# RG-LRU stage of a fused retention / RG-LRU trunk step: next x projection before the gates, gate projection after them, output projection tile by tile

## The reference, cut to what matters

```python
gate_in, x_in = jnp.split(h @ lru_w_in[o], 2, axis=-1)         # two projections, 1024 -> 1024 each
xc = centred_dwconv(x_in, lru_conv_w[o], lru_conv_b[o])         # 4 taps along the tokens, per channel
# rg_lru_dir, once forward and once on the flipped sequence:
r  = sigmoid(block_diag_linear(xc, wa, ba))                     # 8 blocks of 128 x 128
ig = sigmoid(block_diag_linear(xc, wx, bx))
log_a = -LRU_C * r * softplus(-lam)
a, mult = exp(log_a), sqrt(-expm1(2.0 * log_a))
h_t = a_t * h_{t-1} + (mult * (ig * xc))_t                      # a scan along the tokens
mix = (gelu(gate_in) * (h_f + flip(h_b))) @ lru_w_out[o]
x = x + g1 * mix
```

## Time and profile before

| | us |
|---|---|
| three runs | 2728.86, 2735.11, 2736.41 (median 2735.11) |
| the profiled execution, its own time | 2731.88 |
| span of its trace | 2730.1 |
| PE busy in it | 2609.2 (96%) |
| DVE busy | 1641.1 (60%) |
| ACT busy | 666.3 (24%) |
| POOL busy | 699.7 (26%) |

### The profile page before, as it was taken

How to read it: one execution, slowest core, us unless ns; L and a number is a source line. 1 busy time by engine, 2 the same in 40 slices (tenths; PEclk the granted TensorE clock), 3 DMA queues, 4 the chain that set the end, 5 groups by cost and what they waited for, 6 DMA issues and landing times.

```text
span 2730.1 us, 39975 instructions
## 1 busy us (share of the span) xinstructions
PE 2609.2 (96%) x14730; PEld 2524.3 (92%) x14730; DVE 1641.1 (60%) x3056; ACT 666.3 (24%) x1016; POOL 699.7 (26%) x395
## 2 busy tenths in 40 slices
PE   7999999899999999999999889789999999999998
PEld 4999999899999999999998778678999999999997
DVE  5878778548567567567586777855433443442444
ACT  5323323232001001001044544423110110110113
POOL 0221212222222222222223323432222232222321
PEclk9999999999999999999999989899999999999998
DMA  6422222312222222222222101121111111111111
GB/s 235 146 70 69 82 67 71 124 47 66 63 81 69 64 82 69 61 85 69 62 73 104 38 21 36 59 77 31 47 39 42 43 38 46 38 44 41 38 46 70
DMA packets 259139, 181.18 MB, mean 66 GB/s; under 512 B 9205, under 2 KB 253685, under 8 KB 258166
## 3 DMA queue, kind: packets, MB, share of 16 engines
q1 hardware_dynamic: 257924, 169.99, 20.4%
q10 hardware_dynamic: 1138, 10.21, 1.0%
HBM read 165.48 MB, written 14.69 MB: 66 GB/s over the span
## 4 chain that ended last, share of the span: by engine, by line
PE 85%; DVE 9%; issue 3%; ACT 2%; DMA 0%; ACTq 0%; DVEq 0%; POOL 0%; POOLq 0%; SPq 0%
PE psum L588 80%; PE psum L862 2%; DVE mod_sum L1228 2%; DVE work_f L1624 1%; DVE h_lo L1254 1%; DVE sumsq L1197 1%; PE mod_psum L613 1%; DVE x L1275 1%; PE psum L668 1%; DVE sumsq L1260 1%; DVE h_hi L1598 1%; DVE mod_sum L1223 0%; DVE s_bwd L1474 0%; PE psum L743 0%; ACT rate_f L1107 0%
## 5 line engine op out<-in xcount | busy, mean ns | idle before, releaser
L588 PE MATMUL psum<-h_hi,w_hi 128*128 128x384 f32 (+1 forms) x2880 | 682.0, 345 | 36.4 <-DVE h_lo L1254 25.6
L531 POOL CAST w_hi<-w_raw 128x1024 fp32r<-128x1024 f32 x184 | 193.5, 1052 | 1886.9 <-PE psum L588 1041.1
L588 PE MATMUL psum<-h_lo,w_hi 128*128 128x384 f32 (+1 forms) x2880 | 666.1, 340 | 0.0
L588 PE MATMUL psum<-h_hi,w_lo 128*128 128x384 f32 (+1 forms) x2880 | 663.7, 339 | 0.0
L588 PEld LDWEIGHTS psum<-h_hi,w_hi 128*128 128x128 f32 x2880 | 520.2, 191 | 48.7 <-issue 23.3
L1275 DVE SCALAR_TENSOR_TENSOR x<-psum,mod,x 128x768 f32<-128x768 f32 (+2 forms) x432 | 238.5, 610 | 476.8 <-PE psum L588 476.8
L588 PEld LDWEIGHTS psum<-h_lo,w_hi 128*128 128x128 f32 x2880 | 524.4, 190 | 0.0
L588 PEld LDWEIGHTS psum<-h_hi,w_lo 128*128 128x128 f32 x2880 | 521.3, 190 | 0.0
L533 POOL TENSOR_TENSOR w_lo<-w_raw,w_hi 128x1024 fp32r<-128x1024 f32 x184 | 445.6, 2422 | 14.7
L978 ACT ACTIVATE relu<-relu,bias 128x384 f32<-128x384 f32 x128 | 72.0, 610 | 1211.1 <-DVE relu L1326 1211.1
L588 PE MATMUL psum<-hid_hi,w_hi 128*128 128x384 f32 x1536 | 351.8, 336 | 2.8 <-DVE x L1275 2.8
(11 more groups left out here) (223 smaller groups left out, 1886.7 us busy)
## 6 DMA issues: line engine op xcount, KB each, us to landing
w_raw<-in_mlp_w SPq DMA_DIRECT2D x128, 512.0 KB, 4.0
mod_raw<-in_mod_w SPq DMA_DIRECT2D x160, 256.0 KB, 2.9
w_raw<-in_ab_w_in SPq DMA_DIRECT2D x24, 512.0 KB, 4.5
x_spill<-x ACTq DMA_DIRECT2D x2, 4608.0 KB, 13.9
w_raw<-in_lru_w_in SPq DMA_DIRECT2D x16, 512.0 KB, 4.1
x<-x_spill SPq DMA_DIRECT2D x2, 2880.0 KB, 9.6
x_rows<-in_x_sample SPq DMA_DIRECT2D x8, 512.0 KB, 7.4
scale_raw<-in_mod_w SPq DMA_DIRECT2D x8, 512.0 KB, 14.4
```

The source lines that it names most:

```text
L531: pool.tensor_copy(w_hi[:, s, :], w_raw[:, s, :]).then_inc(hi_done, 1)
L588: mm = pe.matmul(psum[:, s, c, 0:end - c * CH], w, v[:, k, c * CH:end], start=(first and n == 0 and w is hi[k] and v is in_hi), stop=(last ...
```

## The change

The order of PE becomes: x projection of block 0; then for each block b: x projection of b+1, gates of b, gate projection of b (the last block has no next x). The convolution accumulates in a tile of its own, `xc_next`; ACT does its first tap with the bias (`conv_start`) and, later in the block, copies `xc_next` to `xc` (`take_xc`), which gates and `block_products` read. DVE begins a block with the convolution of b+1 and evicts the gate projection of b between the two directions. ACT makes `h_hi` of all eight `mix` tiles after its last block; POOL makes the low parts of tiles 0 to 4, DVE those of 5 to 7. `out_proj`, in both layers, does each early input tile for c = 0 and then for c = 1. SP's and POOL's orders follow. Cut to its core:

```diff
-DVE_LOW = 2
+POOL_LOW = 5
+        xc_next = tile_at(9, "xc_next")
...
+            load_unit(None, 0, U1, cols(a["lru_w_in"][0], D_MODEL))
+            with sp.Fori(0, KT - 1) as b:
+                load_unit(b, BLK_UNITS, U1 + 1, cols(a["lru_w_in"][0], b * P + (P + D_MODEL)))
+                load_gates(b)
+                load_unit(b, BLK_UNITS, U1 + 2, cols(a["lru_w_in"][0], b * P))
...
             def block_products(b, last):
-                pool.wait_ge(xc_ready, b + 2)
+                pool.wait_ge(xc_copied, b + 1)
...
             split(first + KT - 1, 0)
+            block_products(KT - 1, True)
             split(first + KT - 1, 1)
-            block_products(KT - 1, True)
+            for k in range(POOL_LOW):
+                low_part(k)
...
+                for n, k in enumerate(order[:KT - late]):
+                    pe.wait_ge(h_ready, H_MIX[l] + n + 1)
                     for c in range(2):
+                        three_passes((I + c) % 2, (k,), parts(w_hi, U + c, KT), parts(w_lo, U + c, KT), h_hi, h_lo,
+                                     first=(n == 0), last=False)
...
-            def lru_block(b):
-                waits = norm_waits(2) if isinstance(b, int) else (None, None)
-                project(b, BLK_ITEMS, I1, BLK_UNITS, U1, *waits).then_inc(unit_done, 1)
-                project(b, BLK_ITEMS, I1 + 1, BLK_UNITS, U1 + 1).then_inc(unit_done, 1)
+            def lru_block(b, last_block):
+                o = 0 if last_block else 1
+                if not last_block:
+                    project(b, BLK_ITEMS, I1 + 1, BLK_UNITS, U1 + 1).then_inc(unit_done, 1)
                 for j in range(4):
...
                     if j == 0:
                         pe.wait_ge(gate_landed, at(b, 64, 64))
-                        pe.wait_ge(xc_ready, b + 2)
+                        pe.wait_ge(xc_copied, b + 1)
...
+                project(b, BLK_ITEMS, I1 + 5 + o, BLK_UNITS, U1 + 1 + o).then_inc(unit_done, 1)
+            project(None, 0, I1, 0, U1, *norm_waits(2)).then_inc(unit_done, 1)
+            with pe.Fori(0, KT - 1) as b:
+                lru_block(b, False)
+            lru_block(KT - 1, True)
...
-                    if l == 1 and n < KT - 1:
-                        continue
...
                     if l == 1:
-                        act.wait_ge(lru_done, 1 + KT)
+                        act.wait_ge(lru_done, 2 + k)
                     act.activation(h_hi[:, k, 0:TOK], mix[:, k, :], ACT.Copy).then_inc(part_hi, 1)
...
+            def conv_start(i, n):
...
+                item_out(act, i, BLK_ITEMS, I0 + n)
                 for c, (start, size) in enumerate(((LPAD, LAT), (CTX0 + LPAD, CTX))):
                     t = xin[:, start:start + size]
                     last = act.activation(t, t, ACT.Identity, bias=bias[:, 0, c:c + 1])
                 last.then_inc(xin_ready, 1)
+                act.wait_ge(xin_ready, b + 1)
+                if n:
+                    act.wait_ge(xc_copied, b)
+                for start, end, row in ((0, LAT, 0), (LAT, TOK, CTX0)):
+                    last = act.activation(xc_next[:, start:end], xin[:, row:row + end - start], ACT.Identity,
+                                          bias=col(par, b + R_CONVB), scale=col(par, b + R_CONVW))
+                last.then_inc(xc_first, 1)
+            def take_xc(i, n):
+                act.wait_ge(xc_ready, at(i, 1, n + 2))
+                if n:
+                    act.wait_ge(gated_ready, at(i, 2, 2 * n))
+                act.activation(xc[:], xc_next[:], ACT.Copy).then_inc(xc_copied, 1)
             def lru_block(b, last_block):                     # ACT
+                if not last_block:
+                    conv_start(b, 1)
                 for j in range(4):                            # the sigmoids, exp, tanh, roots
...
-                    conv_bias(b, 1)
-                item_out(act, b, BLK_ITEMS, I0 + 1)
+                    take_xc(b, 1)
+                item_out(act, b, BLK_ITEMS, I0 + 5 + o)
                 for src, dst in zip(tokens(gate_raw), tokens(gelu_gate)):
...
                 dve.wait_ge(xin_ready, b + 1)
-                if n:
-                    dve.wait_ge(gated_ready, at(i, 2, 2 * n))
-                for j in range(4):
+                dve.wait_ge(xc_first, b + 1)
+                for j in range(1, 4):
...
             def lru_block(b, last_block):                     # DVE
-                if last_block:
-                    dve.wait_ge(lru_done, KT)
-                    for k in range(KT - 1):
-                        dve.tensor_copy(h_hi[:, k, 0:TOK], mix[:, k, :]).then_inc(part_hi, 1)
-                        if k < DVE_LOW:
-                            low_part(k, mix[:, k, :], H_MIX[1], k, TOK)
+                if not last_block:
+                    convolution(b, 1)
                 for d in range(2):                            # lines 1604 to 1609
...
-                if not last_block:
-                    convolution(b, 1)
                 for d in range(2):
+                    if d == 1:
+                        output_gate(b, 0 if last_block else 1)
                     dve.wait_ge(root_ready, at(b, 2, d + 1))
...
-                    if d == 0 and not last_block:
-                        output_gate(b, 1)
...
-                dve.wait_ge(gelu_ready, b + 1)
+                dve.wait_ge(gelu_ready, b + 2)
```

More of the change, by code:

```diff
@@ L540, in block_products @@
             def block_products(b, last):
-                pool.wait_ge(xc_ready, b + 2)
+                pool.wait_ge(xc_copied, b + 1)
                 for d in range(2):
-                    item_out(pool, b, BLK_ITEMS, AT_MIX[1].items + 3 + 2 * d)
+                    item_out(pool, b, BLK_ITEMS, AT_MIX[1].items + (2 if last else 3) + 2 * d)
                     pool.tensor_tensor(gated[d][:], gated[d][:], xc[:], ALU.mult).then_inc(gated_ready, 1)
[L546 to L549, removed]
             first = AT_MIX[1].units // 2 + 1
@@ L778, in out_proj, with tile_ready @@
                 I, U = AT_OUT[l].items, AT_OUT[l].units
-                spans = ((order[:KT - late], True), (order[KT - late:], False))
-                for tiles, early in spans:
+                for c in range(2):
+                    take_set(None, 0, I + c)
+                for n, k in enumerate(order[:KT - late]):
+                    pe.wait_ge(h_ready, H_MIX[l] + n + 1)
                     for c in range(2):
-                        if early:
-                            take_set(None, 0, I + c)
+                        if n == 0:
                             pe.wait_ge(split_done, U + c + 3)
[L786 to L791, removed]
-                        if not early:
-                            mm.then_inc(unit_done, 1)
+                        three_passes((I + c) % 2, (k,), parts(w_hi, U + c, KT), parts(w_lo, U + c, KT), h_hi, h_lo,
+                                     first=(n == 0), last=False)
+                for c in range(2):
+                    def tile_ready(n):
+                        if c == 0:
+                            pe.wait_ge(h_ready, H_MIX[l] + n + (KT - late + 1))
+                    three_passes((I + c) % 2, order[KT - late:], parts(w_hi, U + c, KT), parts(w_lo, U + c, KT), h_hi, h_lo,
+                                 first=False, before=tile_ready).then_inc(unit_done, 1)
                 for c in range(2, KT):
@@ L1123, in lru_block @@
                 last.then_inc(gelu_ready, 1)
-            conv_bias(None, 0)
+            conv_start(None, 0)
+            take_xc(None, 0)
             with act.Fori(0, KT - 1) as b:
@@ L1148, in after @@
                 dve.wait_ge(dve_step, value)
[L1150 removed]
+            for start_at_one in (relu2_ready, hid_ready, gm_out, lru_done, gelu_ready):
                 dve.nop().then_inc(start_at_one, 1)
@@ L1284, in out_proj @@
                 else:
-                    dve.wait_ge(h_ready, H_MIX[l] + KT - 1)
-                    low_part(KT - 1, mix[:, KT - 1, :], H_MIX[l], KT - 1, TOK)
+                    dve.wait_ge(h_ready, H_MIX[l] + POOL_LOW)
+                    for k in range(POOL_LOW, KT):
+                        low_part(k, mix[:, k, :], H_MIX[l], k, TOK)
                 def updated(k):
```

49 lines of the change are left out of this document (21 added, 28 removed).

## The result

The changed kernel takes 2745.85 us (median of 8 runs, 2742.50 to 2752.47) where the kernel before took 2734.74 in the same rounds: ratio 1.0047, 95% interval 1.0033 to 1.0061. It is slower; the lower end of the interval, 1.0033, lies just above the 0.3% that the prediction set as its bound. The profiled execution, the shortest of the eight, took 2742.5 us; its span is 2740.7, 10.6 longer than before.

What follows compares the result with a forecast made beforehand. PE's idle and slow gates behind a late `rate_f`, delayed by DVE's forward scan meeting POOL's split, were taken as the bound. +2.8 + 13.6 - 2.7 = +13.7 on 2731.9 gives 2745.6, stated as 2747 for the median; range 2712 to 2762.

Steps and rivals of the forecast that it cites:

- rival (a): One collision only: block 40.45, 2733 us; second form, DVE between CAST and subtraction: 41.4, 2738; chance 0.28 for both.
- Start: Up to block 0's `gated_b` in the RG-LRU stage: it begins 2.8 us later than before.
- E to g: From DVE beginning to evict the next x (E) to the start of `gated_b` (g), on ACT and PE: 12.2 us.
- the 4.9 us from the third gate to `gated_b`: PE's last two gates in a block: 4.9 us, ends 4.28 and 6.95, with 0.6 left for slow clock.
- Rival (c): PE's clock stays low for third and fourth gate in every block: block 44.85, +12 more, 2759 us; chance 0.12.
- First collision: POOL's first split meets DVE's forward product and scan: 3.35 us lost by DVE, bounds 0 and 3.35.
- Second collision: POOL's second split meets DVE's sum and `mix` product: 2.4 us lost, between 0.92 and 3.35.
- Block: One block of the RG-LRU loop: 42.85 us, 2.27 more than before, +13.6 over six.
- End: From block 6's `gated_b` onward: -7.7 for the step to block 7, +5.0 behind it, together -2.7 us.
- each weight load still goes out about a block ahead: SP's new load order costs nothing, since POOL's splits were released by PE or POOL's own issue, not by loads.
- Output projection, tile by tile: Order of c in the output projection: changes nothing in layer 0; if it waited, about 1.3 us a tile.
- Rival (b): First split misses the forward scan too, so PE binds: block 37.6, whole -24.5, 2709 us; chance 0.18.

Runs made afterwards that it cites:

- experiment 2: Changed kernel with both of POOL's weight splits of a block held until DVE has evicted the next x: ratio 1.0008 to the kernel before.
- experiment 9: Changed kernel with 3 added matmuls on PE ahead of the second gate and 5 ahead of the third: ratio 1.0010 to the kernel before.
- experiment 1: Changed kernel with SP's last two loads swapped, the last gate projection's weights ahead of block 7's gate loads: ratio 1.0026 to the kernel before.
- experiment 5: Changed kernel with both layers' output projections back in the old order, all early tiles for c = 0, then c = 1: ratio 1.0080 to the kernel before.
- experiments 2 and 3: Changed kernel with both splits held until x is evicted, first alone (1.0008), then also with SP's last two loads swapped (0.9984); ratios to the kernel before.
- experiment 12: Changed kernel with SP's loads swapped, both splits and the last split held, 5 added matmuls ahead of the third gate: ratio 0.9930 to the kernel before.
- experiment 6: Kernel before, with POOL's second weight split moved between its two block products in the loop: ratio 0.9931 to the kernel before.
- experiment 8: Changed kernel with 12 added matmuls on PE ahead of the second gate and 9 ahead of the third: ratio 1.0200 to the kernel before.

## Why the prediction was right, and where it was not

The forecast was 2747 us; 2745.85 was measured. The mechanism, that the shifted splits meet DVE's forward scan and its last sum or product head on, is shown by the rows and by experiment 2, which removes both meetings and gets back 2.3 us a block. The total is closer than its terms were. In the blocks, what happened is nearer to rival (a) in its second form (a block of 41.4, the whole +5) than to the forecast; the start and the end cost 5 us more than either had reckoned. That the total fits is luck in good part: 8.0 too much in the loop, 5.1 too little at its ends. Rival (a) too has its block by two errors: 4.3 us of collisions where 3.3 were lost, and 12.2 from E to g where it was 13.2 to 14.8.

- *Start*: +2.8 forecast, +4.8 read from the first x eviction to the first g. The second eviction came 10.7 us behind the first, not 9.5 (taps 5.49 us, and 0.44 for a transfer), and g another 0.8 later than E + 11.5. Read, not tested.
- *E to g*: 12.2 forecast, 13.45 measured in the block shown (13.20 to 14.78 over the six). `rate_f` came at E + 6.2 and the third gate at E + 7.48 as reckoned (6.0 and 7.25). The step that failed is the 4.9 us from the third gate to `gated_b`: it was 5.97. Only 0.6 us of slow clock had been left for the last two gates, on the ground that the second gate goes first; they lost 1.7. The ground doesn't hold: the second gate is slow in two of the six blocks and the last two gates in all, by as much where the second was slow as where it wasn't. That the clock is the cause, experiment 9 shows, since with PE at work E to g is 11.77. Rival (c) was half right: the clock stays partly low in every block, at a price below its 2.0 in all but one.
- *First collision*: 3.35 forecast, 2.70 measured, the same meeting at the same place.
- *Second collision*: 2.4 forecast, 0.61 measured. This is the worst-sized term: DVE came in between CAST and subtraction, and the subtraction waited. Of the prediction's signs of being wrong, POOL's split waiting instead of DVE, half came true here: the split lost 1.53 us. The value had been chosen by a row read as one DVE instruction standing behind both parts of a split. On DVE's timeline there these are two instructions, the first behind the CAST, the next behind the subtraction:

```profile
488.68 1.12 DVE L1228 SCALAR_TENSOR_TENSOR mod_sum<-mod_raw,cond,mod_sum 128x128 f32<-128x128 f32 x1
489.73 2.51 DVE L1228 SCALAR_TENSOR_TENSOR mod_sum<-mod_raw,cond,mod_sum 128x128 f32<-128x128 f32 x1
```

So the row speaks for one wait per instruction, and the lower bound, 0.92, was nearer. The Trainium skill, SBUF — State Buffer, section "Who interferes with whom", lets the later of two such instructions wait for the whole of the other; read instruction by instruction, as rival (a)'s second form did, it is closer to the 0.61 than the 2.4 was, and the 1.0 us that POOL's subtraction lost fits it too.
- *Block*: 42.85 forecast, 41.52 measured, so six blocks cost 5.6 us and not 13.6.
- *End*: -2.7 forecast, +0.4 measured (-2.8 and +3.2). The missing step is the one that was costed at nothing: "each weight load still goes out about a block ahead" holds in the loop and not for its last load, which stands behind a wait for the gates of block 6. It cost 5.7 to 7.8 us (experiment 1), more than the whole miss: without it the step to the last block is 28.27 us, 2.8 below the 31.1 forecast. The low parts behind the gelu cost about what was reckoned: PE began its 144 matmuls 26.35 us behind the last g, about 27 had been forecast.
- *Output projection, tile by tile*: the forecast put no price on the order of c. With POOL's low parts 3.4 us apart (2.6 had been reckoned) it is worth 6.6 us by the profile and 9 by the times (experiment 5).
- *Rival (b)*, PE as the bound, is where the kernel arrives once the splits are held (experiments 2 and 3), at 38.4 to 39.8 a block instead of 37.6, because of the clock: with the wait ahead of the third gate filled as well it is 37.03 (experiment 12).

What the prediction did not see at all is the cheaper road. The collision that it read in the kernel before could be moved by itself: one split behind one product gives 0.9931 without any re-pipelining (experiment 6), and with PE's wait filled too (and the last pair of splits held) the old order stands at 0.9916, the new one at 0.9930. What the re-pipelining takes from PE's wait it gives back in collisions, in a longer way from E to g, and at the ends.

## What to carry to other kernels

Before re-ordering a pipeline, move the one instruction that collides: if DVE waits somewhere anyway (here 5.4 us for tanh), put GpSimd's work beside what precedes that wait. When a queue's order is rewritten, follow its last pass by itself: what goes out "a block ahead" in the loop can stand behind a wait at the end. A short wait of TensorE is priced with the slow matmuls behind it, and a few dummy matmuls that fit the wait can be cheaper than removing it.

## What the runs showed of the hardware that was not expected

- DVE and POOL instructions that meet can take turns: of one meeting DVE paid 2.70 us and POOL 2.34 (1.48 + 4.25 against 1.04 + 2.35), of the next DVE 0.61 and POOL 1.53.
- Six taps of DVE, 4.93 us alone, took 7.29 beside one product of POOL and 12.30 beside a split and two products (experiment 12); DVE's TENSOR_SCALAR with one input took 3.05 instead of 0.76 beside a product of POOL.
- In the changed kernel the same wait of PE ahead of the second gate, 1.9 to 2.5 us, was followed by matmuls at a granted clock of 0.56 and 0.60 in two blocks and 1.00 in four. Behind the next wait, of 2.0 to 3.7 us, it was low in all six (0.57 to 0.74 over the third and fourth gate); with matmuls that nobody needs in both waits, and gaps of 0.47 and 0.59 us left (experiment 9), it was 1.00.
- A gate matmul of 128 x 384 (`xc`, written as f32) takes 0.65 us at full clock (experiment 8), a projection's (`h_hi` and `w_hi`, written as fp32r) 0.19.
